# Hybrid decoder layer, 1 core: value pages of each second sample multiplied on GpSimd and summed on VectorE instead of in TensorE's product with probabilities

## The chip, the core and the metric

The kernel runs on one core of a Trainium2 chip. The metric is the device time of one execution in microseconds. Before the change three runs gave 1752.45, 1756.44 and 1761.77 us, so a median of 1756.44 us. Lower is better. The engines are called TensorE (PE in rows; PEld is its weight load), VectorE (DVE), ScalarE (ACT), GpSimd (POOL) and SyncE (SP, which only issues DMAs here).

## The reference, cut to what matters

One decoder layer: block-sparse attention and a state-space branch beside each other on 256 prompt tokens and 8 samples of one token each, then gates, a projection and a feed-forward network, all float32. The change touches one thing, the attention of the samples. Each of the 8 samples has 1024 past tokens in a paged cache (8 pages of 128 tokens, 16 heads of 64), and its result is the sum over all keys of probability times value:

```python
kb = kp.reshape(b, nb, MOBA_BLOCK, H, d).transpose(0, 3, 1, 2, 4)
vb = vp.reshape(b, nb, MOBA_BLOCK, H, d).transpose(0, 3, 1, 2, 4)
...
s = jnp.where(mask, s, -jnp.inf)
p = jax.nn.softmax(s.reshape(b, H, qc, -1), axis=-1).reshape(s.shape)
return jnp.einsum('bhqkj,bhqkjd->bhqd', p, vs.astype(f32))
```

For a sample this is, per head, a product of 1 x 1024 probabilities with a 1024 x 64 matrix of values: 64 value pages of 128 x 1024 floats (512 KB each) over all samples.

## The kernel before

All large products are one stream of "blocks" on TensorE, numbered b = 0, 1, 2, ... Each block takes 8 tiles of 128 x 128 weights and does three matmuls of 264 columns for each (L1849 to L1851), since a float32 product is made from high and low parts of both operands: 24 matmuls. For block b, ScalarE first rounds the weights to their high half (`w_hi`, L834), VectorE subtracts to get the low half (`w_lo`, L1240), and TensorE starts when that is there (`lo_done`, L1827). ScalarE may round for block b once TensorE has finished block b - 4 (`RING`), so both run at most some three blocks ahead.

Everything else is side work, hung on the same numbers. Each engine walks through all b in order (`drive`) and at step b issues what is listed for that b, waiting for semaphores where needed. The order on every engine is thus fixed by hand through tables of numbers. After step b's `w_lo`, for instance, VectorE does what evacuation, convolution, SSD, keys, softmax, values and states list for b, in that order, and only then turns to `w_lo` of b + 1. SyncE issues the DMAs for b once b blocks are finished.

The samples' attention has three stages. Keys (blocks 30 to 130): GpSimd multiplies each key page by the query (L802, four instructions of 256 columns for a page), VectorE sums over the 64 places of each head (L1468). Softmax (blocks 130 to 153). Values, the stage that the change is in, in 16 value steps at the blocks of `VE` (L340): 155, 160, 166, 171; 177, 182, 187, 192; 198, 204, 209, 214; 220, 225, 229, 233. Each row of four handles two samples (a "group" w); each step m has two halves, and each half one page of either sample (e = 0 and 1). SyncE loads the two pages of a half 6 blocks (first half) or 4 blocks (second half) ahead, into a ring of six page buffers: four called `kv`, two called `more_v`. At the end of block V_AT[m] TensorE does eight matmuls of 512 columns, four for each half (L2076): the weights are 32 columns of probabilities, and the four go to different groups of 32 output partitions of one PSUM tile, `side[3]`. After a group's last step VectorE picks each head's own part with a mask `hmask` (L1230), TensorE adds up over partitions with `bsel` (L2085), and VectorE adds the new token's own part and writes into `attn` (L1535).

Around these, the state-space branch (`SSD` blocks 104 to 182), the states of the samples (`STATE`) and the normalisation of its output (`UN`, blocks 196 to 206, with `x_lo` in L1591 at steps 211 and 212) use the same engines. Block 210 is the first of the product with `w_ssm_out`.

Of the kernel before, what the change touches and what calls it, by code (L numbers as in the profile page):

```python
# [18 lines left out]
ALU = mybir.AluOpType  # L19
# [3 lines left out]
P = 128  # L23
D = 2048
KT = D // P
TP = 256
NB = 8
T = TP + NB
HEADS = 16
# [26 lines left out]
def bass_hybrid_decoder_layer(nc, a, o):  # L56
    ctx = ExitStack()
    with ctx:
# [317 lines left out]
        MASKS = 16  # L376
# [94 lines left out]
        def _(sp):  # L471
# [60 lines left out]
            def value_loads(b):  # L532

                for m in range(16):
                    w, k = m // 4, m % 4
                    for half in range(2):
# [7 lines left out]
                        if k == 1 and half == 0:  # L544
                            wait(sp, vs_mm, w)
# [189 lines left out]
        def _(gp):  # L735
# [34 lines left out]
            for off in (0, 32, 72, 104):  # L770
                drained(gp.affine_select(out=hmask[:, :], in_=hmask[:, :], compare_op=ALU.not_equal, fill=1.0,
                                         base=-off, pattern=[[-1, 8]], channel_multiplier=1))
# [32 lines left out]

            def ends(b):
# [20 lines left out]
            for b in range(END):  # L827
                keys(b)
                ends(b)

# [385 lines left out]
        def _(dve):  # L1216
# [305 lines left out]
            def values(b):  # L1522

                for w in range(4):
                    if b == VE[w][3] + 4:
                        dve.wait_ge(v_mm, 4 * (w + 1))
                        own = hmask[:, :].unsqueeze(2).to_broadcast([P, 8, HD])
                        mul(by_head(value_slot(4 * w + 3, 1, 0)[:, 0:512]), by_head(side[3][:, :]), own).then_inc(vm_done, 1)
                    if b == VE[w][3] + 7:
                        dve.wait_ge(vs_mm, w + 1)  # L1530
                        for h in range(2):
                            bs = slice(2 * w, 2 * w + 2)
                            ts = slice(4 * h, 4 * h + 4)
                            part = side[3][:, 0:16].rearrange("p (k q) -> p k q", q=4)[:, :, 2 * h:2 * h + 2]
                            ins = v.tensor_tensor(attn[:, ts, TP + 2 * w:TP + 2 * w + 2], part, own_t[:, :].rearrange("p (b t) -> p t b", t=AT)[:, ts, bs],  # L1535
                                                  ALU.add)
# [267 lines left out]
        def _(pe):  # L1804
# [256 lines left out]
            def values(b):  # L2061

                for m in range(16):
# [6 lines left out]
                    for half in range(2):  # L2070
                        g = 2 * k + half
                        pe.wait_ge(kv_in[2 * (m % 2) + half], 256 + 32 * (m // 2 + 1))
                        for n in range(4):
                            e, part = n % 2, n // 2
                            first_col = (g * NB + 2 * w + e) * HEADS
                            ins = mm(side[3][32 * n:32 * n + 32, :], sc_flat[:, first_col:first_col + 32],  # L2076
                                     value_slot(m, half, e)[:, part * 512:(part + 1) * 512],
                                     start=(g == 0), stop=(g == NPG - 1), skip_group_check=True)
                    ins.then_inc(v_mm, 1)
                for w in range(4):  # L2080
                    if b == VE[w][3] + 3:
# [119 lines left out]
```

## Time and profile before

| | us |
|---|---|
| median of three runs | 1756.44 (1752.45 to 1761.77) |
| the profiled execution | 1763.49 |
| its span, first to last instruction | 1761.7 |
| TensorE busy in it | 1739.1 (99%) |
| VectorE busy | 1161.6 (66%) |
| ScalarE busy | 901.7 (51%) |
| GpSimd busy | 295.1 (17%) |
| mean granted TensorE clock | 0.994 of full |

A float32 matmul instruction appears as two records in the trace, and matmuls overlap, so a record's length is more than its share of the time; what a piece of work costs TensorE is read from the starts, or from the chain of waits, which gives each piece only the time that it adds. The profiled execution was 7.05 us slower than the median.

### The profile page before, as it was taken

Reading aid. Unit: us, or ns where it says so; the run is one execution under the profiler, and the core shown is the slowest. Engines: PE = TensorE matmul, PEld = TensorE weight load, DVE = VectorE, ACT = ScalarE, POOL = GpSimd, SP = SyncE. Lnnn points to the kernel's source line nnn. Section 1 sums busy time; section 2 is a strip of 40 time slices with the busy share of each in tenths; the row PEclk is TensorE's granted clock in tenths of the full one; section 3 lists DMA queues with packets and bytes.
Section 4 is the critical chain, followed back from the end, with each engine's and each line's share of the span. In section 5 each row is a group of like instructions: output and inputs, shape, how many; then the busy total and the mean of one; then the engine's idle time right before and its main releaser. Section 6 shows DMA issues by size and latency. Waiting matters only on the chain.

```text
span 1761.7 us, 35157 instructions
## 1 busy us (share of the span) xinstructions
PE 1739.1 (99%) x14378; PEld 1698.2 (96%) x14378; DVE 1161.6 (66%) x1727; ACT 901.7 (51%) x1685; POOL 295.1 (17%) x316
## 2 busy tenths in 40 slices
PE   8999999999999999999999999999999999999997
PEld 8999999999998999899999999999999999999997
DVE  6466798899887656845755766666666666445444
ACT  5543466555676657533455645555545554434342
POOL 2165887777000000000000000000000000000000
PEclk8999999999999999999999999999999999999999
DMA  8589988898789999795577486777767676665663
GB/s 248 178 277 313 309 297 279 280 302 297 232 257 345 326 332 307 262 312 190 172 251 221 158 285 218 231 226 223 236 216 240 217 234 201 220 204 187 192 207 98
DMA packets 442561, 430.83 MB, mean 245 GB/s; under 512 B 59696, under 2 KB 418064, under 8 KB 441360
## 3 DMA queue, kind: packets, MB, share of 16 engines
q10 hardware_dynamic: 284480, 285.62, 50.8%
q1 hardware_dynamic: 157760, 142.69, 25.6%
q8 instruction: 113, 1.85, 0.4%
q0 software_dynamic: 160, 0.28, 0.1%
q14 instruction: 48, 0.39, 0.1%
HBM read 406.99 MB, written 21.81 MB: 243 GB/s over the span
## 4 chain that ended last, share of the span: by engine, by line
PE 92%; DMA 2%; SPq 2%; DVE 2%; POOL 0%; issue 0%; ACT 0%; DVEq 0%; ACTq 0%
PE gemm L1849 29%; PE gemm L1850 29%; PE gemm L1851 28%; PE side L2076 2%; DMA kv<-in_cache_k 1%; PE side L1811 1%; SPq L487 1%; DVE w_lo L1240 1%; DMA kv<-in_cache_v 1%; DMA xtok<-in_x_prompt 0%; POOL kv L802 0%; PE side L1977 0%; DMA ex_row<-dt_w 0%; SPq L530 0%; DVE y L1233 0%
## 5 line engine op out<-in xcount | busy, mean ns | idle before, releaser
L1240 DVE TENSOR_TENSOR w_lo<-raw,w_hi 128x1024 fp32r<-128x1024 f32 (+1 forms) x559 | 693.9, 1245 | 532.2 <-ACT w_hi L834 530.6
L1849 PE MATMUL gemm<-x_hi,w_hi 128*128 128x264 f32 x3304 | 948.1, 287 | 5.3 <-DVE w_lo L1240 5.1
L1851 PE MATMUL gemm<-x_hi,w_lo 128*128 128x264 f32 x3312 | 939.3, 284 | 0.0
L1850 PE MATMUL gemm<-x_lo,w_hi 128*128 128x264 f32 x3304 | 937.2, 284 | 0.0
L834 ACT ACTIVATE w_hi<-raw 128x1024 fp32r<-128x1024 f32 (+1 forms) x559 | 582.2, 1044 | 649.4 <-PE gemm L1851 649.1
L1849 PEld LDWEIGHTS gemm<-x_hi,w_hi 128*128 128x128 f32 x3304 | 623.7, 189 | 22.9 <-issue 17.9
L1850 PEld LDWEIGHTS gemm<-x_lo,w_hi 128*128 128x128 f32 x3304 | 624.3, 189 | 0.7 <-issue 0.5
L1851 PEld LDWEIGHTS gemm<-x_hi,w_lo 128*128 128x128 f32 x3312 | 622.4, 188 | 0.0
L802 POOL TENSOR_TENSOR kv<-kv,qb 128x256 f32<-128x256 f32 x256 | 256.5, 1037 | 110.0 <-DMA kv<-in_cache_k 110.0
L1850 PE MATMUL gemm<-g_lo,w_hi 128*128 128x264 f32 x704 | 200.4, 285 | 0.0
L1851 PE MATMUL gemm<-g_hi,w_lo 128*128 128x264 f32 x704 | 199.5, 283 | 0.0
L1849 PE MATMUL gemm<-g_hi,w_hi 128*128 128x264 f32 x704 | 199.4, 283 | 0.0
L1851 PEld LDWEIGHTS gemm<-g_hi,w_lo 128*128 128x128 f32 x704 | 132.6, 188 | 0.0
L1849 PEld LDWEIGHTS gemm<-g_hi,w_hi 128*128 128x128 f32 x704 | 132.6, 188 | 0.0
L1850 PEld LDWEIGHTS gemm<-g_lo,w_hi 128*128 128x128 f32 x704 | 132.1, 188 | 0.0
L1468 DVE TENSOR_REDUCE sc_flat<-kv 128x16 f32<-128x1024 f32 x64 | 77.2, 1206 | 21.0 <-POOL kv L802 21.0
L1849 PE MATMUL gemm<-m_hi,w_hi 128*128 128x264 f32 x256 | 72.8, 284 | 0.0
L1850 PE MATMUL gemm<-m_lo,w_hi 128*128 128x264 f32 x256 | 72.5, 283 | 0.0
L1851 PE MATMUL gemm<-m_hi,w_lo 128*128 128x264 f32 x256 | 72.5, 283 | 0.0
L1849 PEld LDWEIGHTS gemm<-m_hi,w_hi 128*128 128x128 f32 x256 | 48.2, 188 | 0.1
L1850 PEld LDWEIGHTS gemm<-m_lo,w_hi 128*128 128x128 f32 x256 | 48.3, 189 | 0.0
L1851 PEld LDWEIGHTS gemm<-m_hi,w_lo 128*128 128x128 f32 x256 | 48.0, 187 | 0.0
(329 smaller groups left out, 1358.2 us busy)
## 6 DMA issues: line engine op xcount, KB each, us to landing
raw<-in_w_in ACTq DMA_DIRECT2D x99, 1024.0 KB, 7.1
raw<-in_w_gate ACTq DMA_DIRECT2D x44, 1024.0 KB, 5.4
raw<-in_w_up ACTq DMA_DIRECT2D x44, 1024.0 KB, 5.3
raw<-in_w_down ACTq DMA_DIRECT2D x40, 1024.0 KB, 5.6
kv<-in_cache_k SPq DMA_DIRECT2D x64, 512.0 KB, 6.0
kv<-in_cache_v SPq DMA_DIRECT2D x44, 512.0 KB, 6.8
st<-in_state_ssm SPq DMA_DIRECT2D x64, 256.0 KB, 5.5
raw<-in_w_ssm_out ACTq DMA_DIRECT2D x16, 1024.0 KB, 6.3
```

The lines of the kernel that those rows point to most:

```text
L487: sp.dma_start(by_block[q], t[32 * q:32 * q + 32].rearrange("i t (c j) -> i t c j", j=32))\
L802: ins = gp.tensor_tensor(out=page_slot(m)[:, cols], in0=page_slot(m)[:, cols], in1=qb[:, n % 2, cols], op=ALU.mult)
L834: return nc.scalar.activation(out, in_, f, **kw)
L1240: v.tensor_tensor(w_lo[:, s, 0:blk.kts, cols], raw[:, s, 0:blk.kts, cols], rounded(b)[:, 0:blk.kts].bitcast(fp32), ALU.subtract).then_inc( ...
L1468: v.tensor_reduce(out=sc[:, g, n, :], in_=by_head(page_slot(m)), axis=AX.X, op=ALU.add)\
L1811: return nc.tensor.transpose(out, in_, ident[0:k, 0:k])
L1849: mm(out, rounded(b)[:, k], pr.hi[:, x], start=(x == 0), stop=False)
L1850: mm(out, rounded(b)[:, k], pr.lo[:, x], start=False, stop=False)
L1851: ins = mm(out, w_lo[:, s, k, cols], pr.hi[:, x], start=False, stop=(x == pr.kt - 1))
L2076: ins = mm(side[3][32 * n:32 * n + 32, :], sc_flat[:, first_col:first_col + 32], value_slot(m, half, e)[:, part * 512:(part + 1) * 512], s ...
```

## The change

For the sample e = 0 of each pair nothing changes but the width: the four matmuls of a half now take 256 columns each and all serve e = 0, so a half has four matmuls of 256 columns in place of four of 512. For the sample e = 1 GpSimd multiplies each page in place by its probabilities (four instructions of 256 columns; `values` on GpSimd), VectorE adds each page into the running sum of the group (seven adds of 128 x 1024 for a group, 28 in all), and TensorE sums the one page that is left over its 128 keys with `ones` as weights (four matmuls of 256 columns for a group). The loads of SyncE gain a wait for the adds (`k_red`), `hmask` is laid out anew (eight small instructions in place of four), and the last steps of a group follow the new layout.

```diff
@@ SyncE, value_loads
                         wait(sp, v_mm, m - 1 + half)
                         if k == 1 and half == 0:
-                            wait(sp, vs_mm, w)
+                            wait(sp, vs_mm, 2 * w)
+                        elif m > 1 or half:
+                            s = 2 * m + half - 3
+                            if s >= 0:
+                                sp.wait_ge(k_red, NB * NPG + 7 * (s // NPG) + s % NPG + 1)
@@ GpSimd, start
-            for off in (0, 32, 72, 104):
-                drained(gp.affine_select(out=hmask[:, :], in_=hmask[:, :], compare_op=ALU.not_equal, fill=1.0,
-                                         base=-off, pattern=[[-1, 8]], channel_multiplier=1))
+            for n in range(4):
+                for e in range(2):
+                    heads = hmask[:, 4 * e:4 * e + 4]
+                    drained(gp.affine_select(out=heads, in_=heads, compare_op=ALU.not_equal, fill=1.0, base=-36 * n,
+                                             pattern=[[-1, 4]], channel_multiplier=1))
@@ GpSimd, new, called for each b after keys(b) and ends(b)
+            def values(b):
+
+                for m in range(16):
+                    for half in range(2):
+                        if b != V_AT[m] - (3, 0)[half]:
+                            continue
+                        page = value_slot(m, half, 1)
+                        if m == 0 and half == 0:
+                            gp.wait_ge(p_done, 1)
+                        gp.wait_ge(kv_in[2 * (m % 2) + half], 256 + 32 * (m // 2 + 1))
+                        for c in range(4):
+                            cols = slice(c * 256, (c + 1) * 256)
+                            p = sc[:, 2 * (m % 4) + half, 2 * (m // 4) + 1, 4 * c:4 * c + 4].unsqueeze(2)
+                            ins = gp.tensor_tensor(out=by_head(page[:, cols]), in0=by_head(page[:, cols]),
+                                                   in1=p.to_broadcast([P, 4, HD]), op=ALU.mult)
+                        ins.then_inc(k_mul, 1)
@@ VectorE, values
+                for m in range(16):
+                    for half in range(2):
+                        w, g = m // 4, 2 * (m % 4) + half
+                        if b != V_AT[m] + (-1, 2)[half] or g == 0:
+                            continue
+                        page, s = value_slot(m, half, 1), 2 * m + half - 1
+                        dve.wait_ge(k_mul, NB * NPG + 2 * m + half + 1)
+                        if g > 1:
+                            dve.wait_ge(k_red, NB * NPG + 7 * w + g - 1)
+                        v.tensor_tensor(page, page, value_slot(s // 2, s % 2, 1), ALU.add).then_inc(k_red, 1)
                 for w in range(4):
                     if b == VE[w][3] + 4:
-                        dve.wait_ge(v_mm, 4 * (w + 1))
+                        dve.wait_ge(vs_mm, 2 * w + 1)
...
                     if b == VE[w][3] + 7:
-                        dve.wait_ge(vs_mm, w + 1)
+                        dve.wait_ge(vs_mm, 2 * w + 2)
...
@@ TensorE, values
                         for n in range(4):
-                            e, part = n % 2, n // 2
-                            first_col = (g * NB + 2 * w + e) * HEADS
-                            ins = mm(side[3][32 * n:32 * n + 32, :], sc_flat[:, first_col:first_col + 32],
-                                     value_slot(m, half, e)[:, part * 512:(part + 1) * 512],
+                            first_col = (g * NB + 2 * w) * HEADS
+                            ins = mm(side[3][32 * n:32 * n + 32, 0:256], sc_flat[:, first_col:first_col + 32],
+                                     value_slot(m, half, 0)[:, n * 256:(n + 1) * 256],
                                      start=(g == 0), stop=(g == NPG - 1), skip_group_check=True)
                     ins.then_inc(v_mm, 1)
                 for w in range(4):
+                    if b == VE[w][3] + 1:
+                        pe.wait_ge(k_red, NB * NPG + 7 * (w + 1))
+                        for n in range(4):
+                            ins = mm(side[3][32 * n:32 * n + 32, 256:512], ones[:, 0:32],
+                                     value_slot(4 * w + 3, 1, 1)[:, n * 256:(n + 1) * 256], start=True, stop=True,
+                                     skip_group_check=True)
+                        ins.then_inc(vs_mm, 1)
```

Two places of the order. First VectorE, from step 208 to step 214, in the kernel before (`w_lo` is the low half of the weights, `un` and `u` the normalisation, `x_lo` the low half of the input of block 210 and later):

```order
L1240 TENSOR_TENSOR w_lo<-raw,w_hi 128x8x128 x2
L1606 RECIPROCAL un<-un 128x264
L1233 SCALAR_TENSOR_TENSOR u<-u,gains,un 128x264 x2
L1240 TENSOR_TENSOR w_lo<-raw,w_hi 128x8x128
L1606 RECIPROCAL un<-un 128x264
L1233 SCALAR_TENSOR_TENSOR u<-u,gains,un 128x264 x2
L1240 TENSOR_TENSOR w_lo<-raw,w_hi 128x8x128
L1591 TENSOR_TENSOR x_lo<-u,x_hi 128x264 x8
L1606 RECIPROCAL un<-un 128x264
L1233 SCALAR_TENSOR_TENSOR u<-u,gains,un 128x264 x2
L1240 TENSOR_TENSOR w_lo<-raw,w_hi 128x8x128
L1591 TENSOR_TENSOR x_lo<-u,x_hi 128x264 x8
```

And the same place in the changed kernel (L1264 is the old L1240, L1557 the new add):

```order
L1264 TENSOR_TENSOR w_lo<-raw,w_hi 128x8x128
L1557 TENSOR_TENSOR more_v<-more_v,kv 128x1024
L1264 TENSOR_TENSOR w_lo<-raw,w_hi 128x8x128
L1639 RECIPROCAL un<-un 128x264
L1257 SCALAR_TENSOR_TENSOR u<-u,gains,un 128x264 x2
L1264 TENSOR_TENSOR w_lo<-raw,w_hi 128x8x128
L1639 RECIPROCAL un<-un 128x264
L1257 SCALAR_TENSOR_TENSOR u<-u,gains,un 128x264 x2
L1264 TENSOR_TENSOR w_lo<-raw,w_hi 128x8x128
L1557 TENSOR_TENSOR kv<-kv,more_v 128x1024
L1624 TENSOR_TENSOR x_lo<-u,x_hi 128x264 x8
L1639 RECIPROCAL un<-un 128x264
```

Two adds now stand between the `w_lo` of block 208 and the `w_lo` of block 212, both of step 209 of the values; a third follows the `w_lo` of block 213.

Second GpSimd, from the state-space work of step 154 on (`xw`), in the kernel before:

```order
L816 TENSOR_TENSOR xw_85<-xdt,dend 128x256 [waits fin_mm,y_mm,xdt_done,dt_act]
L819 TENSOR_TENSOR xw<-xw_85,cdec 128x256 [waits xw_done]
L824 TENSOR_TENSOR xw_85<-xdt,dend 128x256 [waits xdt_done]
```

and in the changed kernel:

```order
L825 TENSOR_TENSOR kv<-kv,sc_flat 128x256 [waits kv_in0,p_done]
L825 TENSOR_TENSOR kv<-kv,sc_flat 128x256 x3
L839 TENSOR_TENSOR xw_85<-xdt,dend 128x256 [waits fin_mm,y_mm,xdt_done,dt_act]
L842 TENSOR_TENSOR xw<-xw_85,cdec 128x256 [waits xw_done]
L847 TENSOR_TENSOR xw_85<-xdt,dend 128x256 [waits xdt_done]
L825 TENSOR_TENSOR kv<-kv,sc_flat 128x256 [waits kv_in1]
L825 TENSOR_TENSOR kv<-kv,sc_flat 128x256 x3
```

The page products of the values stand in the same queue, so `xw`, for which TensorE waits at the end of block 155, comes behind the first of them.

## Rows read from the trace of the kernel before

**Rows 1.** the page, section 1: busy time, share of the span, instructions.

```profile
PE 1739.1 (99%) x14378; PEld 1698.2 (96%) x14378; DVE 1161.6 (66%) x1727; ACT 901.7 (51%) x1685; POOL 295.1 (17%) x316
```

**Rows 2.** the page, section 4: the chain that ended last, by engine.

```profile
PE 92%; DMA 2%; SPq 2%; DVE 2%; POOL 0%; issue 0%; ACT 0%; DVEq 0%; ACTq 0%
```

**Rows 3.** busy time by stretch: start:end, length, each engine (count), clock, DMA share, GB/s.

```profile
505.00:830.00 325.00, 324.51 (x2709) 296.20 (x2708) 211.96 (x333) 184.26 (x448) 10.93 (x12) 1.00 0.91 299
520.00:540.00 20.00, 19.53 (x160) 17.61 (x159) 17.16 (x28) 17.84 (x55) 1.60 (x3) 1.00 1.08 364
720.00:740.00 20.00, 20.00 (x164) 18.23 (x163) 19.61 (x32) 13.36 (x26) 0.00 (x0) 1.00 0.79 265
740.00:760.00 20.00, 20.00 (x167) 18.43 (x166) 9.46 (x13) 5.98 (x7) 0.00 (x0) 1.00 0.86 285
```

**Rows 4.** instructions of L2076: count, ns minimum/median/maximum, first and last start.

```profile
L2076 PE MATMUL side<-kv,sc_flat x176: 592/592/617, 528.6 to 807.5; 128*32 128x512 f32 x176
```

**Rows 5.** the chain in order of time, 500 to 830 us: start, length, what.

```profile
530.10 1.07 PE side L2076 x8
...
545.87 0.37 PE side L1993 x4
546.23 0.22 PE side L1996 x4
...
548.13 1.85 PE side L2076 x16
...
589.99 0.32 PE gemm L1849
...
598.89 0.79 PE side L2085 x8
...
735.92 0.37 PE gemm L1849
```

**Rows 6.** who waited for whom, 505 to 830 us: total us, times, longest.

```profile
PEld gemm L1849 <- DVE w_lo L1240: 1.0, 2, 0.8
...
PE side L2076 <- DMA kv<-in_cache_v: 0.5, 1, 0.5
```

**Rows 7.** GpSimd's key products, L802: count, ns minimum/median/maximum, first and last start.

```profile
L802 POOL TENSOR_TENSOR kv<-kv,qb x256: 719/740/1800, 104.1 to 432.2; 128x256 f32<-128x256 f32 x128
```

**Rows 8.** GpSimd, 104 to 440 us, by shape: count, busy us, mean ns, idle before.

```profile
L802 POOL TENSOR_TENSOR kv<-kv,qb 128x256 f32<-128x256 f32 x256 | 256.5, 1037 | 110.0 <-DMA kv<-in_cache_k 110.0
```

**Rows 9.** VectorE, 104 to 440 us, by shape.

```profile
L1240 DVE TENSOR_TENSOR w_lo<-raw,w_hi 128x1024 fp32r<-128x1024 f32 x103 | 143.5, 1399 | 34.5 <-ACT w_hi L834 34.2
L1468 DVE TENSOR_REDUCE sc_flat<-kv 128x16 f32<-128x1024 f32 x64 | 77.2, 1206 | 21.0 <-POOL kv L802 21.0
```

**Rows 10.** VectorE, 505 to 830 us, by shape.

```profile
L1240 DVE TENSOR_TENSOR w_lo<-raw,w_hi 128x1024 fp32r<-128x1024 f32 x94 | 115.1, 1226 | 108.9 <-ACT w_hi L834 108.9
```

**Rows 11.** SyncE's value loads, L548: issue to landing.

```profile
DMA to landing us min/median/max: 3.4/6.5/13.1
```

**Rows 12.** timeline of VectorE, 527 to 543 us: start, length, what, idle before.

```profile
530.97 1.23 DVE L1240 TENSOR_TENSOR w_lo<-raw,w_hi 128x1024 fp32r<-128x1024 f32 x1
...
536.11 1.22 DVE L1240 TENSOR_TENSOR w_lo<-raw,w_hi 128x1024 fp32r<-128x1024 f32 x1
```

**Rows 13.** timeline of VectorE, 705 to 740 us.

```profile
711.39 1.23 DVE L1240 TENSOR_TENSOR w_lo<-raw,w_hi 128x1024 fp32r<-128x1024 f32 x1 [2.07 <-ACT w_hi L834]
...
725.36 2.83 DVE L1591 TENSOR_TENSOR x_lo<-u,x_hi 128x264 fp32r<-128x264 f32 x8
...
731.88 2.83 DVE L1591 TENSOR_TENSOR x_lo<-u,x_hi 128x264 fp32r<-128x264 f32 x8
734.64 2.35 DVE L1240 TENSOR_TENSOR w_lo<-raw,w_hi 128x1024 fp32r<-128x1024 f32 x2
```

**Rows 14.** timeline of GpSimd, 0 to 20 us.

```profile
10.72 2.11 POOL L771 TENSOR_SCALAR_AFFINE_SELECT hmask<-hmask 128x8 f32<-128x8 f32 x4
14.28 0.95 POOL L774 MEMSET state_b<- 128x1024 f32 x1 [1.46 <-DMA raw<-in_w_in]
```

More of the change, by code:

```diff
@@ L375, in bass_hybrid_decoder_layer @@
         s2_out = [sem(f"s2_out{s}") for s in range(2)]
-        MASKS = 16
+        MASKS = 20
         def rounded(b):
@@ L829, in _ @@
                 ends(b)
+                values(b)
         @block.scalar
@@ L1529, in values @@
                     if b == VE[w][3] + 7:
-                        dve.wait_ge(vs_mm, w + 1)
[L1531 to L1536, printed above, removed]
+                        dve.wait_ge(vs_mm, 2 * w + 2)
+                        for e in range(2):
+                            n = 2 * w + e
+                            part = side[3][:, 8 * e:8 * e + 8].rearrange("p (k q) -> p q k", k=2)
+                            own = own_t[:, n * AT:(n + 1) * AT].rearrange("p (q k) -> p q k", k=2)
+                            ins = v.tensor_tensor(attn[:, :, TP + n].rearrange("p (q k) -> p q k", k=2), part, own, ALU.add)
                         ins.then_inc(v_cp, 1)
```

## The prediction

> **What bounds the kernel now.** I read four views, from the whole to the place. The page's first section: TensorE is busy 99% of the span, VectorE 66%, GpSimd 17% [rows 1]. The chain of waits: 92% of it is TensorE [rows 2]. So a microsecond of TensorE's stream is worth a microsecond, unless another engine gets late, and work on another engine is free until then. The table by stretch and the list of waits for 505 to 830 us, where the values are done, ask who could get late. TensorE is idle 0.5 of these 325 us, VectorE has 113 us free [rows 3], and TensorE's weight loads waited only 1.0 us for `w_lo` [rows 6]. But the share is an average: VectorE is busy 17.16 of 20 us at 520 to 540, 19.61 of 20 at 720 to 740, and 9.46 in the 20 after [rows 3]. Last the timelines of these two tight places [rows 12, 13]. Clock: 1.00 granted all through (the 2.4 GHz level) [rows 3], so I leave it out.
>
> **What goes from TensorE.** A value step is 8 instructions, 16 records of 512 columns [rows 4], and takes 1.85 us of the chain [rows 5]. The records last 592 ns each, so several run at once: 16 x 0.592 would be 9.5 us. Each of the four column groups gets four records, 2048 columns. The nearest thing with fewer columns is L1996, 4 records of 128 columns in two groups: 256 columns for each group in 0.22 us, 0.86 ns a column [rows 5]. With this slope 1.85 = 0.09 + 2048 x 0.00086. Halved, 0.09 + 0.88 = 0.97 us, a gain of 0.88 a step, 14.1 for 16 steps. Bounds: all of it proportional gives 0.925 and 14.8. If instead records can't come faster than the 8 of the `bsel` sums (0.79 us, 0.099 each [rows 5]), a step costs 1.58 and the gain is 4.3. I take 14.1, since L1996 comes at 0.055 a record and has column groups, as these do, while `bsel` loads the full width.
>
> **What comes to TensorE.** Four `ones` products (one for each group of samples) of 512 columns for each column group: 0.09 + 0.44 = 0.53 us, 2.1 in all (bounds by the same rows 1.9 and 3.2). Their wait for the seventh add is past: VectorE issues it in its step of VE + 2, which it reaches before TensorE begins block VE.
>
> **The first value step.** Its second half waits for its load until 530.10 [rows 5], 0.5 us after the first half [rows 6]. A landing moves with no product, so this step gains only what comes after it, 0.5 of 0.88: +0.4. GpSimd's first page product stands ahead of `xw` for the same place; `xw` gets some 3 to 4 us later, up to 529, but the landing at 530.10 covers it. Without that cover it would cost 1.3.
>
> **GpSimd's products.** 32 pages x 4 instructions. The same shape on key pages takes 0.74 us at the median [rows 7] and 1.037 in the mean, beside a busy VectorE [rows 8]: 3.0 to 4.15 us a page. GpSimd has nearly nothing else. The pages land a median of 6.5 us after issue [rows 11]. A block is (598.89 - 589.99)/3 = 2.97 us [rows 5], so first halves are issued some 17.8 us ahead, land 11 ahead, and are multiplied 7 to 8 ahead. VectorE is at their add (step V_AT - 1) some 10 to 14 us ahead, so it waits up to 3 us there. In the keys VectorE's sums waited 21.0 us for GpSimd over 64 pages [rows 9] and TensorE stayed fed.
>
> **VectorE's total.** 28 adds of 128 x 1024. `w_lo` has that shape and two inputs in SBUF: two of them in a row take 2.35, 1.18 each [rows 13], 33 us in all. The waits: 12 first halves x 3 = 36. Slower while GpSimd works: in the keys `w_lo` took 1.399 us against 1.226 [rows 9, 10], so 103 x 0.173 = 17.8 us for 256 GpSimd instructions, 0.07 for each; 128 give 9 us. Together 78 us of the 108.9 that VectorE spends waiting for rounded weights [rows 10]. On average it fits; what it costs is decided where VectorE has no lead.
>
> **Tight place one, blocks 157 to 160.** The second page is landed at 530.10, multiplied by 533.1 to 534.3, added by 535.5. `w_lo` of block 158, begun at 530.97 before [rows 12], then ends at 536.1 to 536.7; its block starts some 9 us before block 160's matmuls end at 545.87 [rows 5], so at 537.0, or 536.5 with the gain so far. Next, `w_lo` of 160 (begun at 536.11 before [rows 12]) waits for the page of step 160, whose load had landed late as well; I get an end of 542.6 to 543.6 against a start of block 160 at 542.5. Cost 0 to 3, I take 0.7.
>
> **Tight place two, blocks 207 to 213.** VectorE last waits for weights before 711.39; from there to the `w_lo` of block 213, begun at 734.64, no row has an idle time [rows 13]. That `w_lo` ends at 734.64 + 1.18 = 735.8, and TensorE begins block 213 at 735.92 [rows 5]: no slack, VectorE is the bound of this one place. The chain starts from TensorE (the norm's sums, then the rounding), so it moves with it. The change puts two adds into it (after `w_lo` of 208 and of 211): 2.35. TensorE gets there 0.88 earlier (step 209). Some 12 GpSimd instructions fall in: 0.8. Together +4.0 given back; below 2.4 it can't be unless the adds are hidden; without a bound on what GpSimd does to VectorE it is more (rival two). From 740 on VectorE is half idle and nothing more is lost.
>
> On what two engines do to each other the trace has 0.07 us for each GpSimd instruction, above. The Trainium skill, "SBUF — State Buffer", section "SBUF: two separate sides", says that a VectorE instruction with two SBUF inputs and a GpSimd one that reads SBUF lock each other out for a whole instruction, which speaks against this change, as products and adds are both of that kind. By that rule a clash costs the instruction's remaining time; the keys show few such clashes a page, so their mean and the rule can both hold, and only its full price, rival two, would change the sum.
>
> **The rest at nothing.** SyncE's new wait for adds: adds of the page two halves back are done when the load is due, except the second load at block 156, which moves 2 to 3 us and has 5 us in hand; behind it stand the state loads, which have three buffers. `hmask`: eight instructions for four, 2.1 us more (10.72, 2.11 for four), of which 1.46 is idle time before the next one that waits for a DMA [rows 14]; its reader comes at 27 us. The mask product on VectorE now waits one block longer, in time in which it waited for weights anyway.
>
> **The sum.** -14.1 + 2.1 + 0.4 + 0.7 + 4.0 = -6.9 us. On the profiled execution: 1763.49 - 6.9 = 1756.6. That execution was 7.05 above the median, so on the median: 1756.44 - 6.9 = 1749.5, 0.39% less.
>
> **Rivals.** One: the stalls are absorbed, and TensorE's gain shows in full: -14.1 + 2.1 + 0.4 = -11.6, 1744.8. For it: 113 us of free VectorE time, and the keys, with more GpSimd work, hardly stopped TensorE. Against it: no slack at 735.92.
>
> Two, slower: VectorE becomes the bound at both tight places, since each GpSimd instruction holds its two-input instructions for its own full 0.74 us in place of 0.07. 16 such at place two cost 11.8 in place of 0.8 and 8 at place one 5.9 in place of 0.6: -6.9 + 11.0 + 5.3 = +9.4, 1765.8. It decides from about 0.45 us for each, where the gain is eaten up. Against it: in the keys this would have been 256 x 0.74 = 189 us for VectorE where 17.8 are seen. For it: none of those 256 had to be waited for with so little lead.
>
> Three, the change doesn't do what it says: records are paced, not columns (0.099 each). Then -4.3 + 3.2 + 0.4 + 4.7 = +4.0, 1760.4. Against it: L1996.
>
> **How the numbers follow.** My forecast 50%, rival one 25%, rival two 15%, rival three 10%. What a measurement can tell from no change is 0.5%, 8.8 us, so faster means below 1747.7 and slower above 1765.2. The forecast's own range is 1745 to 1754; with the faster bound of a step (0.7) and tight place one at nothing it falls below 1747.7 in three of ten: 0.15. Rival one lies there nearly always: 0.22. Rival two is above 1765.2 in half of its cases: 0.08, rival three in one of ten, 0.01. Faster 0.37, slower 0.09, within 0.54. The range leaves out the far half of rival two and the last of rival one: 1742 to 1764.
>
> **What would show it.** The value steps in the chain at 0.97 us each and the `ones` sums at 0.53; TensorE waiting for `w_lo` some 4 us near block 212 or 213 and below 3 near 158 to 160, and hardly elsewhere; `w_lo` at 1.25 to 1.35 us in the mean; GpSimd's products at 0.75 to 1.04. I am wrong if value steps stay above 1.3 us, if TensorE waits for `w_lo` by more than 8 us in all, if it waits for `xw`, value pages or adds by more than 2, or if a stretch outside 500 to 830 us changes its length.

## The result, and the profile after

The changed kernel is slower: 1763.89 us (13 runs, 1758.89 to 1767.09) against 1756.44 us (13 runs, 1752.45 to 1761.80), a ratio of 1.0033 with an interval of 1.0022 to 1.0044, so 5.8 us. The forecast was 1749.5. In the profiled execution of after (1762.82 us, span 1761.0) TensorE is busy for less time, and the chain that ended last goes through it for less of the span. These rows answer to [rows 1, 2].

```profile
PE 1731.9 (98%) x14410; PEld 1701.8 (97%) x14410; DVE 1209.6 (69%) x1755; ACT 900.7 (51%) x1685; POOL 401.6 (23%) x448
...
PE 83%; DVE 8%; DMA 2%; POOL 2%; issue 2%; ACT 2%; SPq 1%; DVEq 0%; ACTq 0%; POOLq 0%
```

VectorE's share went from 2% to 8%. Where, the stretches show (columns as in [rows 3]).

```profile
505.00:830.00 325.00, 313.79 (x2682) 296.24 (x2681) 255.68 (x354) 180.60 (x436) 116.10 (x140) 0.98 0.90 296
...
690.00:697.00 7.00, 1.39 (x10) 1.21 (x9) 4.92 (x6) 3.66 (x5) 4.35 (x8) 0.87 1.06 350
697.00:702.00 5.00, 5.00 (x22) 4.79 (x22) 4.96 (x6) 2.06 (x4) 1.97 (x2) 0.50 0.29 108
702.00:740.00 38.00, 34.97 (x276) 32.31 (x275) 37.42 (x47) 22.20 (x38) 13.71 (x15) 0.96 0.67 222
```

TensorE is idle for 5.6 of the 7 us from 690. Behind that its granted clock is 0.50 (the 1.2 GHz level) for 5 us, in which 22 matmuls fit, and has gaps again from 702 to 740, where VectorE is full. The chain of after (start, length, what) has the cause.

```profile
592.60 0.79 PE side L2124 x8
...
656.15 1.00 PE side L2108 x16
...
660.26 0.57 PE side L2116 x8
...
666.83 0.79 PE side L2124 x8
...
679.12 0.35 SPq L552
...
680.24 9.38 DMA kv<-in_cache_v
689.68 2.34 POOL kv L825 x4
692.04 1.23 DVE kv L1557
693.27 1.72 DVE un L1639
695.02 1.13 DVE u L1257 x2
696.14 0.34 DVE u_sq L1636
...
738.03 0.39 PE gemm L1882
...
754.78 0.79 PE side L2124 x8
816.41 0.79 PE side L2124 x8
```

A value step (L2108) costs 1.00 us where it cost 1.85 [rows 5]. The `bsel` sums at each group's end (L2124, before L2085) serve as a ruler: they mark the same four places in every kernel of this study. They are 74.23, 87.95 and 61.63 us apart here; in the kernel before 76.87, 76.99 and 64.27 (starts 598.89 [rows 5], 675.76, 752.75, 817.02). Groups 1 and 3 (numbered from 0) gain 2.64 us each, which is four steps at 0.85 less 0.76 for the `ones` products. Group 2, with the same work, loses 10.96, so 13.6 us of stalls lie in it. In group 0 (by the ends of its blocks) stalls of 3.4 eat the gain. Up to the end of block 149 the profile of the kernel before is 6.3 us behind that of after, but also 9.0 behind a second one of its own (`before_again`, below): chance, so only the stretch behind it is compared.

Who waited for whom in after, 500 to 835 us, against [rows 6]:

```profile
DVE w_lo L1264 <- ACT w_hi L858: 38.3, 32, 3.0
DVE kv L1557 <- POOL kv L825: 20.1, 6, 6.7
...
DVE more_v L1557 <- POOL more_v L825: 6.7, 4, 2.3
...
PE side L2136 <- DVE u_sq L1636: 5.6, 1, 5.6
...
PE gemm L1882 <- DVE w_lo L1264: 3.0, 3, 2.2
PE gemm L1882 <- DVE x_lo L1624: 2.3, 1, 2.3
```

The second row's longest, 6.7 us, is the one that counts. VectorE's queue at that place, and what SyncE had issued (start, length, what, idle before):

```profile
692.04 1.23 DVE L1557 TENSOR_TENSOR kv<-kv,more_v 128x1024 f32<-128x1024 f32 x1 [6.74 <-POOL kv L825]
...
700.18 1.63 DVE L1264 TENSOR_TENSOR w_lo<-raw,w_hi 128x1024 fp32r<-128x1024 f32 x1
...
732.34 4.50 DVE L1624 TENSOR_TENSOR x_lo<-u,x_hi 128x264 fp32r<-128x264 f32 x8
```

```profile
674.18 4.13 SPq L618 DMA_DIRECT2D gate_s<-gs_row  x8
679.12 4.53 SPq L552 DMA_DIRECT2D kv<-in_cache_v  x4
```

```profile
696.63 1.22 PE L2136 MATMUL side<-u_sq,ones 128*128 128x264 f32 x2 [5.61 <-DVE u_sq L1636]
...
697.87 0.42 PE L1883 MATMUL gemm<-x_lo,w_hi 128*128 128x264 f32 x1
```

Read together: the loads for step 204 stand on SyncE behind eight loads of gate rows (L618). They are issued from 679.12 on, and the last of the first half lands 9.38 us after its issue at 680.24. GpSimd has multiplied the page by 692.04. VectorE has waited 6.74 us for it, and behind the add in its queue stand the reciprocal, `u` and `u_sq` of the normalisation (the chain above has them from 693.27 to 696.48), for whose sum TensorE waits 5.61 us before it may finish its own side work. Then VectorE runs, with one pause of 0.41 us (for `w_hi`, before 709.09), until the `w_lo` of block 213 is done and TensorE starts it at 738.03. TensorE waits for VectorE again at blocks 210, 212 and 213.

The instructions at the rates that the prediction used, against [rows 7, 8, 10] (count, busy us, mean ns):

```profile
L1264 DVE TENSOR_TENSOR w_lo<-raw,w_hi 128x1024 fp32r<-128x1024 f32 x92 | 119.3, 1299 | 35.1 <-ACT w_hi L858 35.0
...
L825 POOL TENSOR_TENSOR kv<-kv,sc_flat 128x256 f32<-128x256 f32 x88 | 68.7, 810 | 158.6 <-DMA kv<-in_cache_v 158.6
L825 POOL TENSOR_TENSOR more_v<-more_v,sc_flat 128x256 f32<-128x256 f32 x40 | 34.3, 886 | 54.5 <-DMA more_v<-in_cache_v 54.5
```

### The profile page after: what moved, and what is told of

It is laid out like the page before. It is cut to its first block, busy times and chain, and to the rows that moved or that the text cites. A ratio compares the mean times of both kernels' runs of the same rounds, so it can differ in the third digit from the quotient of the medians.

```text
span 1761.0 us, 35428 instructions
## 1 busy us (share of the span) xinstructions
PE 1731.9 (98%) x14410; PEld 1701.8 (97%) x14410; DVE 1209.6 (69%) x1755; ACT 900.7 (51%) x1685; POOL 401.6 (23%) x448
## 3 DMA queue, kind: packets, MB, share of 16 engines
q8 instruction: 113, 1.85, 0.4%
## 4 chain that ended last, share of the span: by engine, by line
PE 83%; DVE 8%; DMA 2%; POOL 2%; issue 2%; ACT 2%; SPq 1%; DVEq 0%; ACTq 0%; POOLq 0%
PE gemm L1882 26%; PE gemm L1883 26%; PE gemm L1884 26%; DVE w_lo L1264 3%; POOL kv L808 2%; DMA kv<-in_cache_v 1%; DMA kv<-in_cache_k 1%; PE side L1844 1%; SPq L487 1%; DVE un L1639 1%; DVE conv_out L1257 1%; ACT w_hi L858 1%; PE side L2108 1%; DMA xtok<-in_x_prompt 0%; DVE u L1257 0%
## 5 line engine op out<-in xcount | busy, mean ns | idle before, releaser
L1264 DVE TENSOR_TENSOR w_lo<-raw,w_hi 128x1024 fp32r<-128x1024 f32 (+1 forms) x559 | 698.4, 1253 | 458.7 <-ACT w_hi L858 456.9
L825 POOL TENSOR_TENSOR kv<-kv,sc_flat 128x256 f32<-128x256 f32 x88 | 68.7, 810 | 158.6 <-DMA kv<-in_cache_v 158.6
L858 ACT ACTIVATE stx<-stx 128x128 f32<-128x128 f32 x128 | 37.9, 298 | 64.6 <-DVE stx L1254 64.6
```

The source lines that it names most:

```text
L825: ins = gp.tensor_tensor(out=by_head(page[:, cols]), in0=by_head(page[:, cols]), in1=p.to_broadcast([P, 4, HD]), op=ALU.mult)
L858: return nc.scalar.activation(out, in_, f, **kw)
L1264: v.tensor_tensor(w_lo[:, s, 0:blk.kts, cols], raw[:, s, 0:blk.kts, cols], rounded(b)[:, 0:blk.kts].bitcast(fp32), ALU.subtract).then_inc( ...
```

## The experiments

Two theories. A: VectorE stands waiting for a late page in front of the normalisation (place 203), and everything behind it is late. B: VectorE has too much work in group 2, from adds and from clashes with GpSimd, and would be late without that wait. "Ruler" is the distance of the sums of groups 1 and 2 in each one's profile, worked out from the chain like the 87.95 above (for gpsimd_adds, whose chain doesn't pass there, from the ends of blocks 195 and 217, which are the same places); ratios are timed against the kernel before on the same chip.

| kernel | median us | ratio [interval] | ruler us |
|---|---|---|---|
| before | 1756.44 | | 76.99 |
| after | 1763.89 | 1.0033 [1.0022, 1.0044] | 87.95 |
| e1_load_first | 1758.70 | 1.0012 [0.9999, 1.0025] | 81.92 |
| e2_small_adds | 1757.47 | 1.0009 [0.9993, 1.0024] | 84.35 |
| e3_small_products | 1755.34 | 0.9999 [0.9985, 1.0012] | 84.48 |
| g013_third_old | 1753.84 | 0.9988 [0.9974, 1.0001] | 76.99 |
| g13_alternate | 1751.18 | 0.9963 [0.9949, 0.9978] | 77.00 |
| gpsimd_adds | 1769.36 | 1.0089 [1.0057, 1.0120] | 87.36 |
| b_late_wait | 1758.69 | 1.0013 [0.9999, 1.0027] | 77.74 |
| b_late_wait_long | 1762.69 | 1.0033 [1.0017, 1.0050] | 83.42 |
| b_adds_only | 1759.56 | 1.0021 [1.0008, 1.0034] | 79.75 |
| b_products_only | 1759.72 | 1.0016 [1.0004, 1.0028] | 79.70 |
| filler_in_stall | 1765.59 | 1.0052 [1.0036, 1.0068] | 88.57 |

**The page earlier (e1_load_first).** Step 204's loads go ahead of the gate rows on SyncE.

```diff
+                if b == UN[0] + 2:
+                    value_loads(b)
                 gate_rows(b)
...
-                value_loads(b)
+                if b != UN[0] + 2:
+                    value_loads(b)
```

> At block 198 SyncE now issues the two value pages of step 204 before the eight gate rows instead of behind them; nothing else differs from the changed kernel. Theory A (the loss sits in one place: the first page of step 204 is landed only at 689.68, VectorE's add waits 6.7 us for it, and the norm's chain behind it holds TensorE until block 213): the page is issued some 5 us earlier, VectorE's wait falls to 0 to 2 us, block 203 loses 2 to 4 us in place of 8.3, and the kernel is 3 to 6 us faster than the changed one, about equal to the kernel before (1.000, from 0.998 to 1.002). Theory B (VectorE and GpSimd slow each other through the whole value stage, the place is accidental): the wait moves elsewhere, at most 1 us is won, 1.003 against before.

The stall at block 203 is gone:

```profile
PE gemm L1885 <- DVE w_lo L1267: 5.7, 4, 2.7
PE gemm L1885 <- DVE x_lo L1627: 2.9, 1, 2.9
PE side L2066 <- POOL xw L850: 1.5, 1, 1.5
PE side L2139 <- DVE u_sq L1639: 1.4, 2, 0.9
```

TensorE waits 1.4 us for `u_sq` in place of 5.6. Counted from the end of TensorE's block 197 the page is there to be multiplied after 8.0 us in place of 15.7: the loads are issued 4.2 us earlier, and they also land in 5.7 to 5.9 us in place of 8.3 to 9.7. The ruler gets 6.0 us shorter, and the times agree in direction (0.21% less than after, which is 3.7 us; theory B's 1.003 lies outside the interval). This profile lost more elsewhere than that of after, above all at blocks 156 (1.5 us for `xw`, the third row), 166 to 171 and 182, which the edit doesn't touch: over the whole stretch it is only 1.4 us ahead. At group 2 it still stands 4.9 us above the kernel before, where 2.6 less were due: 7.6 us of stalls are left, at blocks 206 to 213. So A accounts for some 6 of the 13.6, B for the rest. VectorE, which no longer waits from 690 on, has in this trace what B consists of:

```profile
688.93 0.54 DVE L1619 TENSOR_TENSOR ysam<-ysam,both_t 128x32 f32<-128x32 f32 x1
...
732.02 4.50 DVE L1627 TENSOR_TENSOR x_lo<-u,x_hi 128x264 fp32r<-128x264 f32 x8
```

Four adds stand from 687 to 737, at 1.14 each 4.6 us. Four short instructions like the first row take 0.36 longer than in the kernel before (0.19), 1.4 together; the second `x_lo` group takes 1.67 longer, and seven others (`w_lo` and an add 1.2, `u` and `u_sq` 1.5) 2.7 longer. That is 5.8 for the meetings with GpSimd and 10.4 in all; 2.6 us of lead (b_late_wait, below) go off, and 7.8 are left, where 7.6 are lost.

**Small adds (e2_small_adds) and small products (e3_small_products).** The first adds 8 of 1024 columns, so it leaves most of the running sum out; the second multiplies 2 of each head's 64 columns and leaves the others unmultiplied. Waits and matmuls stay.

```diff
-    v.tensor_tensor(page, page, value_slot(s // 2, s % 2, 1), ALU.add)
+    v.tensor_tensor(page[:, 0:8], page[:, 0:8], value_slot(s // 2, s % 2, 1)[:, 0:8], ALU.add)
```

```diff
-    gp.tensor_tensor(out=by_head(page[:, cols]), in0=by_head(page[:, cols]), in1=p.to_broadcast([P, 4, HD]), ...)
+    gp.tensor_tensor(out=by_head(page[:, cols])[:, :, 0:2], in0=by_head(page[:, cols])[:, :, 0:2],
+                     in1=p.to_broadcast([P, 4, 2]), ...)
```

> The 28 adds work on 8 of 1024 columns each, so the sums over pages of each second sample are left out but for these columns; every wait stays. This takes away the adds' time (28 x 1.1 us of VectorE), not their waits. Theory A with the late page as its main cause: the wait of 6.7 us at step 203 stays, and of the 16 us lost some 5 to 8 come back (three adds in the chain from 692 to 738, the one in step 203, and part of the 3.4 at blocks 160 to 171): 0.999 to 1.000 against before. Theory B, if the adds' time is all: nearly all of the 16 us come back, 0.995. If neither adds nor waits matter but the products' contention: no change, 1.003.

> GpSimd's products work on 2 of each 64 columns, so most of the multiplication of the second sample's values is left out; all waits for landings, all adds and the order stay. A page takes perhaps 0.5 us of GpSimd in place of 2.3 to 4.6. Theory A: the wait at step 203 shortens by the product's time only, 2 us, and with the contention gone in the chain some 2 to 3 us more come back: 1.000 to 1.001 against before. Rival B, lock-out of the two engines as the main loss: 8 us or more come back, 0.998 or lower.

Each alone takes away the stalls of blocks 160 to 171 and some of group 2's (3.6 and 3.5 us of the ruler); in the first 1.5 us for `xw` at the end of block 155 remain. Their times fit theory A (0.999 to 1.000 and 1.000 to 1.001 expected) and rule out the other values on record. Each keeps the stall at 203: TensorE's wait for `u_sq` is 4.5 us in the first and 3.8 in the second. So that stall needs neither the adds' nor the products' length; it is there by the page's landing alone. `w_lo` takes 1.268 us in the mean in the first and 1.235 in the second, against 1.299 in after and 1.226 before [rows 10].

**Some groups only (g013_third_old, g13_alternate).** The new way for groups 0, 1, 3 or for 1 and 3; the others as before.

```diff
+    NEW = (1, 3)
...
-    if b != V_AT[m] - (3, 0)[half]:
+    if b != V_AT[m] - (3, 0)[half] or m // 4 not in NEW:
```

> Groups 0, 1 and 3 of the samples are done in the new way, group 2 (steps 198 to 214) in the old way, all in TensorE with 512 columns. Theory A: the whole loss from block 203 to 213 (8.3 + 2.9 + 1.1 + 0.4 = 12.7 us) goes, and with it group 2's gain of 4 x 0.85 - 0.77 = 2.6 us: net 10 us faster than the changed kernel, some 4 to 5 us faster than the kernel before, 0.997 (0.996 to 0.998). Theory B, general contention: a quarter of the change is gone, so a quarter of the loss, 1.002.

> Groups 1 and 3 of the samples in the new way, groups 0 and 2 in the old one. If the loss sits only where VectorE has no lead (group 0: blocks 160 to 171; group 2: blocks 203 to 213), both places are as before and groups 1 and 3 keep 2 x (4 x 0.85 - 0.77) = 5.3 us, so TensorE should not wait for VectorE near steps 177 to 192 and 220 to 233 and the kernel is 5 us faster than before: 0.997 (0.996 to 0.998). If contention costs everywhere, half of the change keeps half of the loss: 1.0015.

With group 2 old the ratio is 0.45% (7.9 us) below that of after, and group 2's loss of 10.96 is gone from the ruler. Against the kernel before, 4 to 5 us were expected; its profile gains 4.5 over the stretch, but timed it is 0.12%, some 2 us, which can't be told from nothing. Group 0 keeps its stalls there (TensorE waits 1.5 us for `xw` and 1.7 for a `w_lo`). With groups 1 and 3 alone it beats both kernels by more than the interval: 1751.18. TensorE is then never idle in the whole stretch:

```profile
505.00:830.00 325.00, 325.00 (x2762) 303.32 (x2761) 235.86 (x352) 184.53 (x436) 63.01 (x76) 1.00 0.91 301
```

Two groups at 2.64 give 5.3 us; timed are 0.37%, 6.5 us (3.9 to 9.0).

**Adds on GpSimd (gpsimd_adds).** GpSimd sums the pages as well; VectorE has no add and no wait for pages.

```diff
+    gp.tensor_tensor(out=page[:, cols], in0=page[:, cols], in1=value_slot(s // 2, s % 2, 1)[:, cols], op=ALU.add)
...
-    v.tensor_tensor(page, page, value_slot(s // 2, s % 2, 1), ALU.add).then_inc(k_red, 1)
```

> The 28 adds move from VectorE to GpSimd (four instructions of 256 columns each, behind the page's products); VectorE neither adds nor waits for a page. Theory A (the late page held VectorE and the adds lengthened its chain): all stalls of blocks 160 to 213 go but for what GpSimd's reads slow VectorE's two-input instructions (1.63 in place of 1.22 us in the changed kernel's trace when products run beside them), now for twice as many GpSimd instructions: 2 to 4 us lost of the 10.5 gained, 6 to 8 us faster than before, 0.996. Rival (the two engines' contention is the main loss): it doubles, 1.004 or more.

Missed, and in the other direction: the slowest of all. Part of it is GpSimd's own lateness: TensorE waits 3.8 us for its last sums of a group (L837, in two groups) and 2.3 for `xw`. More is VectorE's. The edit doubles the instructions on GpSimd that meet VectorE's, and VectorE pays for them in its work with two SBUF inputs (last figure before the bar: mean ns):

```profile
L1276 DVE TENSOR_TENSOR w_lo<-raw,w_hi 128x1024 fp32r<-128x1024 f32 x91 | 130.7, 1439 | 61.4 <-ACT w_hi L870 61.4
...
L1626 DVE TENSOR_TENSOR x_lo<-u,x_hi 128x264 fp32r<-128x264 f32 x16 | 12.0, 818 | 0.0
```

`w_lo` 1.439 us and `x_lo` 0.818 against 1.226 and 0.424 in the kernel before. The adds went off VectorE, but what its other instructions gained in length keeps it the late engine of group 2.

**Each suspect by itself in the kernel before.** First the wait alone: at step 203 VectorE waits for the landing of step 204's first half (b_late_wait) or second half (b_late_wait_long), and nothing else changes.

```diff
+    if b == V_AT[9] - 1:
+        dve.wait_ge(kv_in[2], 256 + 32 * 5)    # kv_in[3] in b_late_wait_long
```

> The kernel before with one wait added and nothing else: in step 203 VectorE waits until the two pages of step 204's first half are landed, as the changed kernel's add in effect does. In the trace of before they land some 3.3 us after VectorE gets to step 203. Theory A: the chain from there to block 213 has no slack at its end, so TensorE loses 3 to 4 us near blocks 202 to 213: 1.002. Rival (a wait there is absorbed by the lead of 6.5 us that w_lo of block 203 has): nothing, 1.000.

> The kernel before with one wait added: in step 203 VectorE waits for the landing of the second half's pages of step 204 instead of the first half's, in the trace of before 3.5 us later, so VectorE stands some 6.8 us in place of 3.3. If the norm's product in block 202 has about 3 us of lead over VectorE, and only what goes beyond it counts, TensorE now waits 3.5 to 4.5 us there, and loses up to 2.7 more by its clock: 5 to 7 us at block 203, 1.003 to 1.004, where the 3.3 us cost 0.75. Rival (the 8.3 us of the changed kernel need the product and the adds beside it): 1 to 2 us.

The first wait is 3.3 us long and costs the ruler only 0.75: VectorE had 2.6 us of lead, so my expectation of 3 to 4 us missed. The second is 6.9 long, as in after, and then it costs 6.43:

```profile
697.12 1.80 DVE L1608 RECIPROCAL un<-un 128x264 f32<-128x264 f32 x1 [6.87 <-DMA kv<-in_cache_v]
```

```profile
PE side L2099 <- DVE u_sq L1605: 4.0, 1, 4.0
```

```profile
697.00:702.00 5.00, 1.65 (x5) 1.47 (x6) 4.84 (x6) 2.28 (x4) 0.00 (x0) 0.62 1.08 373
702.00:710.00 8.00, 8.00 (x59) 7.20 (x61) 7.52 (x10) 1.74 (x4) 0.00 (x0) 0.81 0.07 26
```

(b_late_wait_long: VectorE's timeline, TensorE's wait, and two stretches with the clock as the third figure from the right.) TensorE stands for 4.0 us, and the other 2.4 are the time at the lower clock (the clocks of the two stretches are means: up to 704.88 its matmuls start 0.22 us apart, then 0.12). In the kernel before nothing is late behind this place, so a wait that exceeds the lead by some 4 us is paid once, with the clock on top.

Then the work alone. b_adds_only adds three sums of 128 x 256 at each of steps 203, 208 and 211 of VectorE; b_products_only has GpSimd multiply when the pages of the value steps of blocks 204, 209 and 214 have landed, 24 instructions on a buffer that no other engine reads any more.

```diff
+    if b in (203, 208, 211):
+        dve.wait_ge(fin_out, 16 * NG)
+        for c in range(3):
+            drained(v.tensor_tensor(hfin[:, :, :], hfin[:, :, :], hfin[:, :, :], ALU.add))
```

```diff
...
+    for c in range(4):
+        p = upper[:, 4 * c:4 * c + 4].unsqueeze(2).to_broadcast([P, 4, HD])
+        page = by_head(hfin[:, :, :].rearrange("p a b -> p (a b)"))
+        ins = gp.tensor_tensor(out=page, in0=page, in1=p, op=ALU.mult)
```

> The kernel before with three small additions of 128 x 256 in a row, some 1.3 us together, on a free buffer in each of steps 203, 208 and 211 of VectorE, in the places of three of the new adds, with no wait for GpSimd and no product. My prediction's term: the two of steps 208 and 211 lengthen a chain without slack, the one of 203 falls into idle time: TensorE loses 2.6 us at blocks 212 and 213, 1.0015. Rival (the adds' time is hidden too, only waits and contention count): nothing, 1.000.

> The kernel before with GpSimd's products of steps 209 and 214 and of step 204 (6 pages, 24 instructions) at their places in time, but on a small buffer of their own of 128 x 256, their results unused; VectorE neither waits for them nor adds. It measures what GpSimd's reads cost VectorE alone. By the mean of the keys (0.07 us for each GpSimd instruction) 1 us or less at blocks 210 to 213, by the changed kernel's trace (two-input instructions of VectorE 0.41 us longer when they meet one) 2 to 4 us: 1.001 to 1.002.

Both came as expected: 2.76 us of the ruler for the adds (those of steps 208 and 211, 1.34 us each; the one of step 203 fell into idle time) and 2.71 for products that no engine waits for. The latter cost VectorE time in place two, where it has none to give:

```profile
727.18 4.49 DVE L1611 TENSOR_TENSOR x_lo<-u,x_hi 128x264 fp32r<-128x264 f32 x8
```

Eight `x_lo` take 4.49 us in place of 2.83. GpSimd does four instructions beside them, so each costs VectorE 0.41.

**Is the lower clock to blame? (filler_in_stall)** Twelve extra matmuls at the end of TensorE's block 202 of the changed kernel keep TensorE at work while it would stand; nothing reads them.

```diff
+    if b == 202:
+        for _ in range(12):
+            mm(u_psum(g)[:, 0:TP], ones[:, :], cmask[:, :], start=True, stop=True)
```

> The changed kernel with twelve matmuls of 256 columns (ones with a constant, some 5.3 us at full clock) on TensorE at the end of block 202, just ahead of its wait for the norm's sum; their result is overwritten by that product. They fill the time in which TensorE stands still there. If the loss of 8.3 us in block 203 is 5.6 us of waiting and some 2.7 us because TensorE's granted clock is 0.5 after it (its matmuls come every 0.22 us in place of 0.12 from 697 to 702), the clock stays at 1.0 and 2 to 3 us come back: 1.0015 to 1.002 against before. Rival (the slow matmuls after the wait come from VectorE, GpSimd or memory traffic beside them): nothing comes back, 1.003 or worse.

```profile
690.00:697.00 7.00, 6.98 (x37) 5.94 (x36) 5.16 (x6) 3.80 (x6) 4.10 (x8) 1.00 1.06 353
697.00:702.00 5.00, 5.00 (x43) 5.00 (x42) 4.96 (x6) 2.05 (x4) 2.06 (x2) 1.00 0.29 111
702.00:740.00 38.00, 32.14 (x248) 29.00 (x247) 37.83 (x47) 22.38 (x38) 13.80 (x15) 0.96 0.67 222
```

The clock stays at 1.00 and 43 matmuls fit where 22 did. At block 203 itself 2.8 us come back, as expected. But the ruler is 88.57, no shorter than the 87.95 of after, and the time isn't better: the expectation missed. From 702 to 740 TensorE is busy for 32.14 us in place of 34.97: what it won it waited for later. VectorE started late here too, at 691.81, and had no pause up to the end, so it alone set the end of this place. The lower clock of after ran in its shadow, but for the one pause of 0.41 us.

**The kernel before once more (before_again).** Unchanged, one profile, as the yardstick for the part ahead of block 150.

> The kernel before, unchanged, for a second profile of it. In its first profile TensorE waited for VectorE in blocks 47 to 66, with the clock at 0.5 once, which no other kernel's profile shows; if this is chance, the second profile ends some 6 us earlier before block 150, and from block 150 on it is the same as the first within 0.5 us.

One execution took 1753.83 us, 9.7 less than the first profiled one; the ruler read 77.00 (76.99). Of the 9.7, 9.0 lie ahead of block 150 (6 expected), and 0.6 at block 156, where the load of the first value step landed earlier. So the first profile carries microseconds of chance, none of them in groups 1 to 3.

## Why the prediction was wrong

Its numbers ran from 500 to 830 us; there the sum was -6.9, and the blocks' ends in the two profiles give +5.7: -10.6 from TensorE's instructions, -0.7 at the first value step, +3.4 in group 0 and +13.6 in group 2. The timed 5.8 bears that out.

**TensorE's side was right.** A value step measured 1.00 us against 0.97, the gain 0.85 against 0.88; the `ones` sums 0.57 in the chain against 0.53, with their neighbours 0.76. Together -10.6 against -12.0 (the same two terms). Rival three, paced records, falls. The first value step's +0.4 isn't seen: its load landed early enough in this execution, which is chance (0.6 of it is in `before_again` too). That execution was lucky once more: `xw` was ready at 520.64 and TensorE took it at 521.24. In e1_load_first, e2_small_adds, g013_third_old and filler_in_stall TensorE waits 1.5 us for it there. The prediction knew this cost (1.3) and set it at nothing because the landing at 530.10 would cover it; that cover isn't always there.

**The step that failed** is "VectorE is at their add (step V_AT - 1) some 10 to 14 us ahead, so it waits up to 3 us there", whose waits were costed at nothing for TensorE. It took the median landing, 6.5 us [rows 11], for each page, though 13.1 stood in the same row, and it never looked at what the loads stand behind on SyncE nor at what stands behind the add on VectorE. The sum of the waits was not too small (26.8 us against 36); one of them, 6.7 us, stood in front of the norm's sum and cost 8.3 us at block 203: 5.6 of TensorE standing, 2.7 at the lower clock. By itself in the kernel before, such a wait cost 6.4 (b_late_wait_long); with the page earlier the changed kernel got 6.0 back (e1_load_first); the other 2.3 of the 8.3 it lost at the blocks behind instead. Its sign of being wrong, TensorE waiting "for `xw`, value pages or adds by more than 2", came true indirectly: TensorE waited for `u_sq`, which stood behind an add.

**Tight place two** was the right place with too small a price: 4.0 forecast; 13.6 measured, of which 7.6 remain with the page on time. Its adds were right (2.35 for two; their stand-ins in b_adds_only cost 2.76). Wrong was the clash, 0.07 us for each GpSimd instruction. It was a mean taken from the `w_lo` alone and spread over all 256 products. One that meets a `w_lo` makes it 1.63 us in place of 1.22, one that meets the `x_lo` costs the same 0.41. In e1_load_first the meetings cost VectorE 5.8 us at this place, where 0.8 stood; only 1.2 of them fell on instructions of the size of `w_lo`, 4.5 on `x_lo`, `u`, `u_sq` and the short ones, for which the prediction had no term. Nor did the prediction count the adds of steps 203 and 206, which stand in the same run of work: four, not two, come before the `w_lo` of block 213.

**Tight place one** was forecast at 0.7 (0 to 3); group 0 lost 3.4, of which 0.9 at blocks 160 to 166 and 2.5 at block 171, which the prediction didn't name. Adds and products decide there together, since small ones of either kind take these stalls away.

**Rival two** had the sign and the mechanism but not its price: 0.74 for each of 24 instructions was taken, 0.41 for those that meet is measured. It gave 1765.8, near the time, but that is luck: some 6 us of what was lost came from the late page. Its point of decision, 0.45 for each, should have been 0.35 by its own numbers (24 x 0.35 less the 1.4 already in the sum is about the gain of 6.9); the 5.8 us of e1_load_first are 0.24 for each of the 24 product instructions that ran at that place. The prediction had weighed a rule of the Trainium skill, "SBUF — State Buffer", section "SBUF: two separate sides": a VectorE instruction with two SBUF inputs and a GpSimd one that reads SBUF lock each other out, whoever is first holds for its whole instruction. The traces agree with the kind: only instructions with two SBUF inputs grow (the reciprocal keeps 1.79 us), and GpSimd's grow as well, to 0.810 and 0.886 in the mean. They show 0.41 us as the usual price to VectorE of a meeting, less than a whole product instruction (0.58 us each when four take 2.34).

Why 0.41, the traces on record settle. A start and a length for GpSimd and for the `w_lo` that began beside it, twice in the kernel before and once in after (the `w_lo` of 700.18 above):

```profile
241.14 0.73 POOL L802 TENSOR_TENSOR kv<-kv,qb 128x256 f32<-128x256 f32 x1
241.70 1.25 DVE L1240 TENSOR_TENSOR w_lo<-raw,w_hi 128x1024 fp32r<-128x1024 f32 x1
...
348.45 0.74 POOL L802 TENSOR_TENSOR kv<-kv,qb 128x256 f32<-128x256 f32 x1
348.45 1.82 DVE L1240 TENSOR_TENSOR w_lo<-raw,w_hi 128x1024 fp32r<-128x1024 f32 x1
```

```profile
700.03 0.71 POOL L825 TENSOR_TENSOR more_v<-more_v,sc_flat 128x256 f32<-128x256 f32 x1 [4.58 <-DMA more_v<-in_cache_v]
```

GpSimd's instruction had 0.17, 0.74 and 0.56 us left, and `w_lo` took 1.25, 1.82 and 1.63: 1.08 us and the rest. That holds within 0.01 us for all 71 `w_lo` of the keys in the kernel before (104 to 440 us) that began with 0.15 us or more of a GpSimd instruction left, and in all profiles of this study together, from 104 to 835 us, for 1172 of 1191. In the 19 others GpSimd's instruction was itself drawn out to end 1.28 us or more later, and `w_lo` took its usual 1.22. So the price is the rest of the instruction under way less 0.14 us; 0.41 is what it comes to where two engines take turns and some 0.55 is left each time. A mean price depends on how the starts fall, and can't be carried from one stretch to another. Nor does VectorE always pay. In e1_load_first the first eight `x_lo`, begun 0.17 us ahead of a product, took their 2.83 us, and the product took 3.13:

```profile
725.42 3.13 POOL L828 TENSOR_TENSOR kv<-kv,sc_flat 128x256 f32<-128x256 f32 x1 [7.74 <-DMA kv<-in_cache_v]
```

**What isn't settled:** how adds and meetings share group 0's 3.4 us, since either alone costs nothing there; why the first eight `x_lo` kept GpSimd out to their end while the second eight took turns with it; and why the loads of step 204 also land faster when they go ahead of the gate rows.

## What to carry to other kernels

Before an engine is made to wait, list what is queued behind that instruction and who waits for it, and take the landing of that very load with what its queue issues first, not the median of the line. A contention price that is a mean over a stretch holds only there; where an engine has no lead, take the price of one meeting, up to the length of the other engine's instruction, for every instruction of the kind that pays. And if a change gains in some stages and loses in one, try it without that one: two groups of four kept 5.3 us, all four lost 5.8.

## What the hardware showed

- After 5.6 us without work TensorE's granted clock was 0.50 (1.2 GHz) for some 5 us, its matmuls of 264 columns 0.22 us apart instead of 0.12; around 4.0 us of standing (b_late_wait_long) it was 0.62 from 697 to 702 and 0.81 from 702 to 710, means of that level and the full one. In the second kernel that was paid in full (2.4 us), in the first hardly at all, since another engine was the later one.
- A VectorE instruction of 128 x 1024 with two SBUF inputs takes 1.22 us alone and 1.63 beside a GpSimd product, and one of 128 x 32 takes 0.54 where it takes 0.19 alone: nearly the same addition for very unlike lengths. The addition is what is left of the GpSimd instruction under way, less 0.14 us (0.03 to 0.60 us for the `w_lo` of the keys). `x_lo` goes from 0.354 to 0.562 each where four products fall on eight.
- Four groups of matmuls with 32 output columns each ran side by side: 16 records of 512 columns cost 1.85 us, 16 of 256 columns 1.00 us.
